# A hybrid attention and mixture-of-experts block: the high-part products of a weight piece ahead of the wait for its low part, a later first gate, filler products and earlier bias products

## What is computed

```python
def _moe(h, w_router, b_router, w1, b1, w2, b2):
    logits = (t @ w_router + b_router)
    top_v, top_i = lax.top_k(logits, TOP_K)          # 4 of 32 experts per token
    top_w = jax.nn.softmax(top_v, axis=-1)
    ...
    def expert_rows(args):                           # a block of 128 rows of one expert
        xe, e = args
        hh = xe @ w1[e] + b1[e]                      # 1024 -> 2048
        glu = jnp.minimum(hh[:, :D_FF], SWIGLU_LIMIT)
        lin = jnp.clip(hh[:, D_FF:], -SWIGLU_LIMIT, SWIGLU_LIMIT)
        act = glu * jax.nn.sigmoid(SWIGLU_ALPHA * glu) * (lin + 1.0)
        return act @ w2[e] + b2[e]                   # 1024 -> 1024
    ...
# y = RMSNorm(x + attention + moe)
```

## Time and profile before

| | before |
|---|---|
| median of 3 runs | 1501.88 us (1500.56 to 1502.05) |
| profiled execution | 1504.46 us, of it 1502.7 us from the first to the last instruction |
| PE busy | 1456.1 us, 97% |
| DVE busy | 1339.3 us, 89% |
| ACT busy | 1113.2 us, 74% |
| POOL busy | 259.4 us, 17% |
| granted TensorE clock, mean | 0.992 of 2.4 GHz |
| HBM read | 445.18 MB, 311 GB/s with the writes over the span |

### The profile page before, as it was taken

One profiled execution on the slowest core, in us unless ns is written; L12 is line 12 of the kernel. 1 busy time (PEld: TensorE's weight loads), 2 busy tenths in 40 slices (PEclk: granted clock), 3 DMA queues, 4 the chain that ended last, 5 costly groups with the idle time before them and its releaser, 6 DMA issues.

```text
span 1502.7 us, 22310 instructions
## 1 busy us (share of the span) xinstructions
PE 1456.1 (97%) x7031; PEld 1176.1 (78%) x7031; DVE 1339.3 (89%) x1534; ACT 1113.2 (74%) x1345; POOL 259.4 (17%) x199
## 2 busy tenths in 40 slices
PE   6999999998999999999999999999999999999996
PEld 5777787786888888888888787888888888888874
DVE  5678756569999999999999999999999999999997
ACT  5668555346788888887888888888888888887885
POOL 5000000135111111111211111222211111111110
PEclk9999999979999999999999999999999999999998
DMA  8021022359999999999999999999999999999963
GB/s 241 27 84 57 29 93 66 127 205 417 376 370 366 367 364 375 379 370 375 360 373 367 365 369 369 367 367 373 367 362 376 357 373 369 364 365 377 374 223 122
DMA packets 100216, 451.82 MB, mean 301 GB/s; under 512 B 13459, under 2 KB 25747, under 8 KB 67409
## 3 DMA queue, kind: packets, MB, share of 16 engines
q1 hardware_dynamic: 90848, 434.68, 76.5%
q0 software_dynamic: 9328, 16.64, 4.6%
HBM read 445.18 MB, written 22.54 MB: 311 GB/s over the span
## 4 chain that ended last, share of the span: by engine, by line
PE 64%; DVE 21%; issue 8%; ACT 5%; DMA 1%; POOL 1%; DVEq 0%; POOLq 0%; SPq 0%; ACTq 0%
PE zpair L2138 42%; DVE stage_lo L1190 8%; PE bank L2138 7%; ACT stage_hi L773 3%; DVE qk L1613 2%; DVE act_lo L1573 2%; PE bank L1752 2%; PE bank L1848 2%; DVE qk L1609 2%; PE bank L1754 2%; PE bank L1753 2%; PE bank L2097 2%; DVE lbuf L1267 1%; PE zpair L2108 1%; DVE pt_lo L1276 1%
## 5 line engine op out<-in xcount | busy, mean ns | idle before, releaser
L1190 DVE TENSOR_TENSOR stage_lo<-ring,stage_hi 128x1024 fp32r<-128x1024 f32 x796 | 951.4, 1222 | 47.1 <-ACT stage_hi L773 11.1
L773 ACT CAST stage_hi<-ring 128x1024 fp32r<-128x1024 f32 x796 | 828.0, 1053 | 187.5 <-PE zpair L2138 143.2
L2138 PE MATMUL zpair<-stage_hi,act_hi 128*128 128x512 f32 x1024 | 323.0, 397 | 3.4 <-DVE stage_lo L1190 3.2
L2138 PE MATMUL zpair<-stage_lo,act_hi 128*128 128x512 f32 x1024 | 316.7, 390 | 0.0
L2138 PE MATMUL zpair<-stage_hi,act_lo 128*128 128x512 f32 x1024 | 316.1, 390 | 0.0
L2138 PEld LDWEIGHTS zpair<-stage_hi,act_lo 128*128 128x128 f32 x1024 | 192.2, 188 | 41.4
L2138 PEld LDWEIGHTS zpair<-stage_hi,act_hi 128*128 128x128 f32 x1024 | 186.8, 188 | 48.0 <-DVE stage_lo L1190 11.9
L2138 PEld LDWEIGHTS zpair<-stage_lo,act_hi 128*128 128x128 f32 x1024 | 192.2, 188 | 41.1
L659 POOL COPY sidx<-gtab 128x1 int32 (+1 forms) x31 | 110.1, 3552 | 394.8 <-ACT qk L1080 394.8
L2138 PE MATMUL bank<-stage_hi,act_hi 128*128 128x512 f32 x512 | 165.0, 404 | 4.2 <-DVE stage_lo L1190 0.7
L2138 PE MATMUL bank<-stage_lo,act_hi 128*128 128x512 f32 x512 | 158.6, 391 | 0.0
(11 more groups left out here) (311 smaller groups left out, 1431.3 us busy)
## 6 DMA issues: line engine op xcount, KB each, us to landing
ring<-in_w SPq DMA_DIRECT2D x384, 1024.0 KB, 7.6
ring<-in_w_in SPq DMA_DIRECT2D x12, 1024.0 KB, 5.3
ring<-in_w_out SPq DMA_DIRECT2D x4, 1024.0 KB, 4.9
xs_all<-in_x SPq DMA_DIRECT2D x4, 512.0 KB, 7.6
ring<-in_x SPq DMA_DIRECT2D x4, 512.0 KB, 3.7
tn_scratch<-qk SPq DMA_DIRECT2D x4, 512.0 KB, 3.4
x_scratch<-ring SPq DMA_DIRECT2D x4, 512.0 KB, 3.8
ring<-x_scratch SPq DMA_DIRECT2D x4, 512.0 KB, 5.8
```

What stands on the lines that cost most here:

```text
L773: nc.scalar.copy(dst, src).then_inc(split_hi, 1)
L1190: nc.vector.tensor_tensor(dst, src, hi_ap.bitcast(F32), ALU.subtract).then_inc(split_lo, 1)
L2138: mm = pe.matmul(bank[b0 + h][:], w[:, k, :], m[:, j % STAGES, h * BANK:(h + 1) * BANK], start=start and w is T_hi and m is stage_hi, stop ...
```

## The change

- In `multiply` the order of the three pairs of products becomes high x high, low x high (`T_lo` with `stage_hi`), high x low (`T_hi` with `stage_lo`). The first waits for ACT's high part (`split_hi`); the wait for the low part stands ahead of the third pair.
- In the first body, ACT's gate function moves from behind piece 2 to behind piece 4, DVE's first clip from behind piece 1 to behind piece 0, and the gated product from behind piece 3 to behind piece 5.
- Six unread products are issued ahead of the logits of the last tile, and the four behind the weight table become 18.
- The second biases of three tiles are multiplied ahead of the count's load and branch. In the branch's overflow part they are cleared and made again.

```diff
@@ ACT, run_items, body
                                 x_evac(q0 + 1)
+                        if j == 4 and first:
                             gate(q0)
@@ DVE, run_items, body
-                        if j == 1 and first and b == MOE0:
+                        if j == 0 and first and b == MOE0:
                             clip_first(1)
...
-                        if j == 3 and first:
+                        if j == 5 and first:
                             gated(q0)
@@ PE
             turn_x2(7)
+            keep_busy(5, 6)
             logits(3)
@@ PE, multiply
-                pe.wait_ge(split_lo, at)
-                for (w, m) in ((T_hi, stage_hi), (T_hi, stage_lo), (T_lo, stage_hi)):
+                pe.wait_ge(split_hi, at)
+                for (w, m) in ((T_hi, stage_hi), (T_lo, stage_hi), (T_hi, stage_lo)):
+                    if m is stage_lo:
+                        pe.wait_ge(split_lo, at)
                     for h in range(2):
                         mm = pe.matmul(bank[b0 + h][:], w[:, k, :], m[:, j % STAGES, h * BANK:(h + 1) * BANK],
-                                       start=start and w is T_hi and m is stage_hi, stop=stop and w is T_lo)
+                                       start=start and w is T_hi and m is stage_hi, stop=stop and m is stage_lo)
@@ PE, run_items
                     weight_table()
-                    keep_busy(0, 4)
+                    keep_busy(0, 18)
                     pe.wait_ge(counts_read, 1)
@@ PE, end
             run_items(MAIN)
+
+            def second_biases(t, start=True):
+
+                for h in range(2):
+                    pe.matmul(bank[FIN[t] + h], wdT[0:96, t * P:(t + 1) * P], b2r[0:96, h * BANK:(h + 1) * BANK], start=start, stop=not start)
+            pe.wait_ge(b2_lo, 1)
+            pe.wait_ge(y_ready, E - 1)
+            for t in range(3):
+                second_biases(t)
             pe.wait_ge(over_ready, 1)
             n_over = pe.value_load(novi[0:1, 0:1], min_val=0, max_val=OVER)
             with pe.If(n_over > 0):
+                for t in range(3):
+                    second_biases(t, False)
                 pe.wait_ge(y_ready, E)
                 pe.wait_ge(onehot_r, 2 * TT)
                 run_items(REST)
                 pe.wait_ge(y_ready, ITEMS)
...
+                for t in range(3):
+                    second_biases(t)
...
-            pe.wait_ge(b2_lo, 1)
-            pe.wait_ge(y_ready, E - 1)
-            for t in range(3):
-                second_biases(t)
             pe.wait_ge(onehot_r, TT)
             pe.wait_ge(y_ready, E)
```

More of the change, by code:

```diff
@@ L2224, in _ @@
                 pe.wait_ge(y_ready, ITEMS)
-            def second_biases(t):
-                for h in range(2):
-                    pe.matmul(bank[FIN[t] + h], wdT[0:96, t * P:(t + 1) * P], b2r[0:96, h * BANK:(h + 1) * BANK], start=True, stop=False)
+                for t in range(3):
+                    second_biases(t)
             def last_expert(t):
```

## The result

The changed kernel took 1486.78 us (median of 4 runs, 1485.24 to 1489.88), the one before 1501.97 in the same job. The ratio is 0.9897, with an interval of 0.9884 to 0.9910: 15.2 us less. A second job gave 1486.80 against 1504.21, ratio 0.9886 (0.9870 to 0.9901). The forecast was 1483.0 in a range of 1477.5 to 1491.0: the direction and the large term are right, and 3.8 us of the expected gain are missing.

A forecast was written before the change was run, and what follows sets the result against it. PE and DVE were taken to take turns, PE holding 64% of the wait chain. Terms 12.0 + 3.1 + 3.0 + 0.8 = 18.9 us off the median 1501.88 gave 1483.0 us, range 1477.5 to 1491.

The forecast's parts named there:

- The wait behind four products: Every item, piece 22: PE's 0.40 us loss to the late low part goes under four products; 12.0 us over 30 items.
- The first body: First body: later gate ends DVE's 1.46 us idle; later low-part use gives 0.91, unused lead 0.7; 3.1 us.
- Eighteen fillers for four: Ahead of the first gather's landing: fillers keep PE's clock up for transposes, fillers and first piece; 3.0 us.
- Six fillers: Ahead of the last logits: fill PE's 0.73 us gap to hold the clock; at most 1.57, taken as 0.8 us.
- The early biases: Kernel's end: bias products move under PE's stand, but DVE's wait for the sums' load hides it; 0 us.
- A: Rival at both filler places: the fillers don't hold the clock; 1486.8 us, chance 0.18.
- B: Rival, steady stretch gives its gain back: whole (DMA limit) 1495.0, 0.08 together with D; half 1489.0, 0.09.
- C: Rival in all 768 pieces: a wait inside a piece delays loading the next weights; 1587 us, chance 0.05.
- D: Rival in `multiply`: both waits end up at a piece's first product; 6.9 us left, chance 0.08 with B's whole.

The follow-up runs named there:

- e1: Kernel before with only the new order of products and the low-part wait ahead of the third pair: 1489.57 us, ratio 0.9905.
- e6: Changed kernel, new order of products kept, but the wait for the low part at the start of a piece: 1500.52 us, ratio 0.9983.
- e7: Changed kernel with the old order of products and the low-part wait ahead of the second pair, so two products cover it: 1487.27 us, ratio 0.9897.
- e3: Changed kernel with the first body's gate function, first clip and gated product back in their old places: 1490.04 us, ratio 0.9914.
- e4: Changed kernel without the six fillers and with four instead of eighteen behind the weight table: 1487.80 us, ratio 0.9900.
- e8: Changed kernel with four of five additions left out in each of POOL's two overflow-table sums: 1484.69 us, ratio 0.9877.
- b2: Changed kernel without the six fillers and with 12 instead of 18 behind the weight table: 1486.76 us.
- e2: Changed kernel with the old `multiply` (old order, wait at a piece's start), all other edits kept: 1500.38 us, ratio 0.9980.
- b1: Changed kernel with POOL's first overflow-table sum moved ahead of the second gather: 1486.82 us.

## Why the prediction was right, and where it was not

*The wait behind four products, 12.0 us: right.* The item is 35.14 (forecast 35.15), the 29 items gave 12.16 and the written-out one 0.43 more. e1 shows that it needs nothing else, e6 that it is the place of the wait, e7 that 0.45 of cover is nearly enough. Going by the starts and not by PE's share of busy time was the decision that mattered: the share would have said 3.5.

*The first body, 3.1 us: right in sum, partly by luck.* 1.0 from the order of products (e1) and 2.0 from the later gate (e3), to piece 8. My split was 0.9 and 1.46 + 0.7. But both e1 and e3 have a stand of over 2 us and a fall of the clock behind it that the changed kernel is spared (0.47 us there). The prediction had no such term, and how much of the 2.0 it is stays open.

*Eighteen fillers for four, 3.0 us: this step failed.* What I summed, 0.90 + 1.15 + 0.90, is there at the first piece: 2.9 (e4). The step "it is on the path: DVE then idles until PE has released a stage buffer" was true of the kernel before and not of the one after. With PE faster, that idle time is gone, the 3.39 us of e4, and in its place DVE and POOL work side by side and slow each other. From there DVE is the bound, and 1.33 of the 2.9 arrive at piece 8. I had asked what covers the fillers, and not what is late next. By e8 POOL's first sum is 0.76 of what is lost; the rest is DVE without idle time to give.

*Six fillers, 0.8 us: the size not shown, and the reason partly wrong.* I took the 3.60 us logits as the rule; they are one of several outcomes (1.97 to 3.60). What the fillers do reliably is to keep the clock up through the logits and the four fillers behind them; after that it falls all the same. The means give 1.3 us at the table and 0.8 at the transposes, the latter inside their scatter, and no median shows either (b2 without the six: 1486.76 against 1486.80). The queue ahead of the transposes, whose end I had placed 0.2 us ahead of the gather's landing, mostly ends behind it.

*The early biases, 0: right within the measurement*, though the cover is thin.

*The sum.* 12.6 + 3.0 + 1.3 + 0.8 = 17.7 us, against medians that are 15.2 and 17.4 apart. From 1501.88 it gives 1484.2, and 2.6 us are still missing to 1486.8. e2 points at the small parts: 4.1 by the places in the profiles, 2.6 in the medians, though 4.1 is within its interval (1.7 to 4.4). Runs of one kernel differ by 2 to 6 us. Between the profiles of different kernels the start of the last logits varies by 0.8 us and the part behind the 29 items from 66.5 to 69.1 us, the longest in e4, where PE's stand at the branch is 3.75, so what one profile shows there is one draw. That rest stays open. So 12.6 us are shown for the wait behind four products, and 1.7 to 4.4 for the other edits together.

*The rivals.* A is false for both gaps: with the six the logits, and with eighteen or twelve the transposes, run at 1.00 in each profile, though in between the clock falls in all ten profiles with the six: in the changed kernel the 22 fillers take 3.69 us for 2.58. The Trainium skill ("TensorE: Matmul & The Clock Gate", Why this matters for your kernels) ties a drop to longer idle gaps of PE than these; the runs do not bear that out, the transposes behind 1.5 to 1.7 us of idle time take 1.94 us, those of a clock of 0.50, in each of three kernels (before, e1, e4). But its time, 1486.8, is the one measured: from outside, a gain that is taken back looks like a gain that never came. By the time alone A would have won over the forecast of 1483.0; only the profiles tell them apart. B is false: the loads flow at 373 GB/s. C is false: a satisfied wait in the middle of each of 768 pieces costs nothing that the spacing of 0.45 shows. D is false by the place of the wait in e6.

## What to carry to other kernels

When an engine waits for one operand of several, put the work that needs only the early operands first and the wait where the late operand is first read; a wait that is mostly satisfied cost nothing in the middle of a group here. Size such a gain from the spacing of starts, and count it only as far as the next engine: ask who bounds the stretch once the wait is gone. For stages whose length varies from run to run, read several profiles, or a ratio of two kernels' medians, before a single row is taken as the rule.

## What the runs showed of the hardware that was not expected

- The size of what DVE and POOL cost each other: 2.29 or 6.76 us for the same five additions (e4, the changed kernel), 0.62, 1.6 or 9.48 us for the same multiplication (b1), and 1.16 or 1.46 us for a low part.
- In the steady stretch the same 114 instructions of POOL are busy for 192.59 us in the kernel before and 273.73 after. Nearly all of it is two of them: the issue of the scatter (L663) takes 4.22 us for 1.82, and the copy ahead of it (L659) 4.02 for 3.63. It goes with the place of PE's wait (e1 and e7 as after, e2 and e6 as before) and no wait for POOL shows in the stretch; the cause stays open.
- The granted clock fell to 0.50 behind a gap of 0.73 us among narrow products in two of four kernels within 0.6 us, and in the other two 2 us later, with no gap in between. Six unread products in the gap kept it up through the logits in all ten, and it fell within some 10 us all the same. In the first body a stand of 2.14 us left it at 1.00 in the kernel before, and one of 2.14 or 2.15 was followed by 0.50 in e1 and e3.
